# Six projections of a decoder block as seven half-matrix products each, with the weight sums shared by GpSimd and VectorE

## The chip, the core and the metric

The kernel runs on one core of a Trainium2 chip. The metric is the device time of one execution in microseconds (us), as the median of several runs. The engines are TensorE (PE, its weight loads PEld), VectorE (DVE), ScalarE (ACT), GpSimd (POOL) and SyncE (SP), which here only issues DMAs. Each engine works through its own list of instructions in order; semaphores tie the lists together.

## The reference: what is computed

One decoder block for 256 tokens of width 1024, all in float32:

```python
h = rms_norm(x, g_mix)
(qa, ka, va, za, beta, a, qd, kd, vd, gate_a, gate_b) = split(h @ w_in)
oa = gated_delta_rule(l2(silu(conv(qa))), l2(silu(conv(ka))), silu(conv(va)), beta, a)
oa = rms_norm(oa, g_delta_out) * silu(za)
od = rms_norm(diff_attention(norm(qd), norm(kd), vd, lam, rel_bias), g_subln) * (1 - lam_init)
x  = x + (sigmoid(gate_a + b0) * oa + sigmoid(gate_b + b1) * od) @ w_o
x  = x + moe(rms_norm(x, g_ffn))      # top 4 of 32 experts, 1024 -> 2048 -> 1024
```

The change is in the projections qd, kd, vd (attention), za (Z), gate_a and gate_b. Each is h (256 x 1024) times a 1024 x 1024 part of w_in.

## The kernel before, in words

The program has a **front** (all up to the router) and an **expert stage** (32 experts, two per turn of a loop).

Front, first part: 24 *tiles* (L1420) compute q, k and v of the delta rule, transposed, 128 channels at a time; VectorE does the convolution of each tile (L980, L982, L990). Between the last tiles stand the four `kq` steps (L1479 on TensorE; mask products L1067 and L1069 on VectorE).

Front, second part: 48 *half items* `pj` (L1430). Two of them make one quarter result: 128 tokens x 512 columns, eight chunks of 128 channels accumulated in one PSUM bank. A half item is four float32 matmuls, which the profile shows as eight records. They are TensorE's filling: the table `after`, filled by `put(i, ...)`, says which step of the other work each engine does behind item i. The steps that the prediction speaks of:

- `sb`: inversion of 64 triangular 32 x 32 blocks on VectorE, 31 steps of two instructions (L1084, L1085) in eight pieces behind items 3 to 10. At its end (semaphore `s_tc`) SP stores the blocks to DRAM (L496) and loads them back turned (L502, eight DMAs). The first matmuls of the delta rule that use them are `n2` (L1395), behind item 11.
- `nq`, `nk`: the norms of qd and kd on VectorE: a sum over 64 columns (L1115, L1121), a reciprocal, a root on ScalarE, and four small steps (`roots`). `ktd` turns kd on TensorE (L1528); it needs `nk`.
- `y1`, `y2`, `y3`, `yt`, `s1`, `ks`, `o0`, `qs`, `o1`: the delta rule, TensorE L1395, taken by VectorE or ScalarE.
- per attention head h: `a1` (logits; row maximum on VectorE L1182 to L1187, exp on ScalarE L828), `aw` (weights, VectorE L1192 to L1200), `a2` (turn them on TensorE, L1548), `a3` (times the values).
- `odn`, `oan`: norms and gains of both outputs on VectorE; `mt`: turning of the mix; then the four products with w_o (L1574).

SP's queue loads w_in in pieces of 2 MB into ring slots 8, 9 and 6 in turn. As slots of the front die it loads the experts' weights, in slabs of 2 MB: slabs 0 to 4 in the front, 5 to 10 around the product with w_o. From slab 11 on a slab waits until the experts have used the slot (L425). GpSimd has little to do in the front: constants, bias terms, four squares (L643), two squares (L647), and the gain on oa (L652).

Of the kernel before, what the change touches and what calls it, by code (L numbers as in the profile page):

```python
# [11 lines left out]
ALU = mybir.AluOpType  # L12
# [3 lines left out]
P = 128  # L16
# [20 lines left out]
def block_kernel(nc, x, g_mix, w_in, b_gate, conv_w, a_log, dt_bias, g_delta_out, q_norm, k_norm,  # L37
# [17 lines left out]
    NPIECE = 2 * len(GROUPS)  # L55
# [53 lines left out]
    put(9, ("qt", 0))  # L109
    put(10, ("qt", 1), ("nq",))  # L110
# [44 lines left out]
    ROOTS = ["x", "k", "qd", "kd", "oa", "od", "r0", "r1"]  # L155

    ctx = ExitStack()
    with ctx:
# [71 lines left out]
        junk = ring[:, 7, 2 * D:3 * D]  # L230
# [5 lines left out]
        xT = ring[:, 2, 2 * D:].rearrange("p (c t) -> p c t", c=KC)  # L236
        rr_rows = ring[:, 1, 0:T]
# [78 lines left out]
        s_ss, s_tr, s_xT, s_hT = sem("row_squares"), sem("transposes_done"), sem("scaled_xT_blocks_ready"), sem("hT_halves_ready")  # L316
# [4 lines left out]
        s_pj, s_pjf = sem("projections_done"), sem("projections_taken")  # L321
        s_conv, s_sig, s_silu = sem("conv_done"), sem("conv_tanh_done"), sem("silu_done")
# [20 lines left out]
        s_gbl = sem("gate_bias_loaded")  # L343
        s_gs, s_gm, s_gd = sem("gate_tanh_done"), sem("gate_product_done"), sem("gain_product_done")
# [44 lines left out]
        def _(sp):  # L389
# [1414 lines left out]
```

## Time and profile before

| | |
|---|---|
| median of 3 runs | 1275.73 us (1274.88 to 1276.53) |
| span of the profiled execution | 1273.7 us, so 2.0 us below the median |
| TensorE busy | 1229.8 us (97%), granted clock 0.999 of full speed |
| VectorE busy | 373.2 us (29%) |
| ScalarE busy | 284.8 us (22%) |
| GpSimd busy | 45.9 us (4%) |
| DMA | 451.94 MB |
| chain that ended last | TensorE 66%, DMA 19%, VectorE 5%, ScalarE 3% |

The profile is of one execution. Its page gives the busy times, the span in 40 slices, the chain of work that ended last, and the costliest groups of instructions. The whole-span shares mix two stages with different limits, so each stage has to be read by itself. A busy TensorE is not a TensorE at its peak; that a busy share of 97% leaves no idle time says nothing on what each instruction is for.

### The profile page before, as it was taken

The page shows a single profiled execution, that of the slowest core. Times are in us where ns is not written, and L with a number is a line of the kernel's source. Part 1 is how long each engine was busy: PE and PEld are TensorE (multiplying, and loading weights), DVE is VectorE, ACT ScalarE, POOL GpSimd, SP SyncE. Part 2 cuts the span into 40 slices and gives each one's busy share as a digit, 9 for nine tenths or more (in the row PEclk, how much of TensorE's full clock was granted, in tenths as well). Part 3 has the DMA queues.
Part 4 walks back from the last instruction along what each step waited for, and adds up shares of the span by engine and source line. Part 5 has one row for each costly group of instructions (what it writes and reads, how often), then busy time and mean ns, then how long its engine had stood idle before and what let it go on. Part 6 is the DMA issues. An engine that isn't in the chain of part 4 may idle for free.

```text
span 1273.7 us, 14917 instructions
## 1 busy us (share of the span) xinstructions
PE 1229.8 (97%) x5590; PEld 539.1 (42%) x5590; DVE 373.2 (29%) x1063; ACT 284.8 (22%) x573; POOL 45.9 (4%) x100
## 2 busy tenths in 40 slices
PE   9999999999999999999999999999998989999997
PEld 7777466644443333333333333333333333333332
DVE  5766825666231211111221111221111112211111
ACT  3331212352222121121121112121121211121121
POOL 4400000101000000000000000000000000000000
PEclk9999999999999999999999999999999999999999
DMA  7653431567779999999999999999999999999997
GB/s 255 181 164 129 147 134 67 181 248 264 274 284 417 425 429 429 429 428 430 429 428 427 429 428 428 428 429 429 429 428 428 428 428 429 429 429 429 428 427 314
DMA packets 60764, 451.94 MB, mean 355 GB/s; under 512 B 10600, under 2 KB 13800, under 8 KB 36032
## 3 DMA queue, kind: packets, MB, share of 16 engines
q1 hardware_dynamic: 59176, 447.44, 85.2%
q0 software_dynamic: 1120, 3.56, 1.0%
q10 hardware_dynamic: 440, 0.58, 0.1%
q8 instruction: 16, 0.26, 0.1%
q14 instruction: 12, 0.10, 0.0%
HBM read 449.21 MB, written 1.97 MB: 354 GB/s over the span
## 4 chain that ended last, share of the span: by engine, by line
PE 66%; DMA 19%; DVE 5%; ACT 3%; issue 1%; SPq 1%; DVEq 0%; ACTq 0%
PE pb L1719 20%; DMA space<-in_w_up_dram 19%; PE pb L1766 14%; PE pb L1430 11%; PE pb L1660 4%; PE pb L1420 3%; PE pb L1647 3%; PE pb L1574 2%; PE pb L1395 2%; PE pb L1654 1%; PE pb L1679 1%; DVE buf_a L1334 1%; DVE buf_a L1331 1%; DVE buf_a L1328 1%; ACT buf_a L898 1%
## 5 line engine op out<-in xcount | busy, mean ns | idle before, releaser
L1719 PE MATMUL pb<-space,buf_a 128*64 128x512 f32 x2048 | 460.4, 595 | 15.5 <-DMA space<-in_w_up_dram 15.4
L1719 PEld LDWEIGHTS pb<-space,buf_a 128*64 128x64 f32 x2048 | 146.1, 137 | 284.8 <-issue 257.3
L1766 PE MATMUL pb<-space 128*64 128x512 f32 x1024 | 227.1, 595 | 7.3 <-ACT space L905 7.3
L1328 DVE TENSOR_SCALAR buf_a<-pb 128x256 f32<-128x256 f32 x64 | 27.0, 421 | 686.7 <-PE pb L1719 686.7
L1430 PE MATMUL pb<-space 128*128 128x512 f32 x384 | 171.4, 594 | 0.0
L1766 PEld LDWEIGHTS pb<-space 128*64 128x64 f32 x1024 | 70.7, 137 | 140.9 <-issue 125.3
L1430 PEld LDWEIGHTS pb<-space 128*128 128x128 f32 x384 | 70.3, 190 | 76.1 <-issue 75.1
L881 ACT ACT_TABLE_LOAD x32 | 41.1, 1283 | 222.5 <-PE pb L1647 222.5
L1420 PE MATMUL pb<-space 128*128 128x256 f32 x384 | 88.6, 384 | 0.9 <-ACT space L734 0.5
L1420 PEld LDWEIGHTS pb<-space 128*128 128x128 f32 x384 | 71.3, 190 | 13.1 <-issue 2.4
L898 ACT ACTIVATE buf_a<-buf_a 128x256 f32<-128x256 f32 x64 | 26.7, 417 | 216.7 <-DVE buf_a L1328 216.7
L1660 PE MATMUL pb<-space 64*128 64x512 f32 x264 | 65.6, 615 | 0.8 <-ACT space L907 0.8
L907 ACT COPY space<-pb 128x512 f32<-128x512 f32 x32 | 18.7, 585 | 209.8 <-PE pb L1766 209.8
L1647 PE MATMUL pb<-xt,plan 128*64 128x512 f32 x248 | 58.7, 592 | 0.0
L898 ACT ACT_TABLE_LOAD x32 | 41.1, 1283 | 0.6
L905 ACT COPY space<-pb 128x256 f32<-128x256 f32 x64 | 24.4, 382 | 70.1 <-PE pb L1679 70.1
L982 DVE SCALAR_TENSOR_TENSOR space<-space 128x255 f32<-128x255 f32 (+2 forms) x72 | 36.3, 504 | 2.6
L1647 PEld LDWEIGHTS pb<-xt,plan 128*64 128x64 f32 x248 | 18.9, 137 | 34.3 <-issue 34.3
L1660 PEld LDWEIGHTS pb<-space 64*128 64x128 f32 x264 | 22.8, 186 | 23.1 <-issue 23.1
L1395 PEld LDWEIGHTS pb<-space 128*128 128x128 f32 x240 | 29.0, 192 | 6.2 <-issue 6.2
L1331 DVE TENSOR_TENSOR buf_a<-buf_a 128x256 f32<-128x256 f32 x64 | 27.2, 425 | 9.7 <-ACT buf_a L898 6.7
L1334 DVE SCALAR_TENSOR_TENSOR buf_a<-buf_a 128x256 f32<-128x256 f32 x64 | 27.3, 426 | 7.9
(299 smaller groups left out, 807.3 us busy)
## 6 DMA issues: line engine op xcount, KB each, us to landing
space<-in_w_up_dram SPq DMA_DIRECT2D x127, 2048.0 KB, 25.7
space<-in_w_down_dram SPq DMA_DIRECT2D x61, 2048.0 KB, 24.2
space<-in_w_in_dram SPq DMA_DIRECT2D x17, 2048.0 KB, 8.0
space<-in_w_o_dram SPq DMA_DIRECT2D x2, 2048.0 KB, 11.9
space<-in_w_down_dram SPq DMA_DIRECT2D x4, 1024.0 KB, 27.3
space<-in_w_down_dram SPq DMA_DIRECT2D x4, 512.0 KB, 16.0
space<-in_w_up_dram SPq DMA_DIRECT2D x2, 1024.0 KB, 41.1
xt<-in_x_dram SPq DMA_DIRECT2D x2, 512.0 KB, 5.3
```

Of the source, the lines that this page charges most:

```text
L881: sc.copy(xgt, pb[:, 3, :]).then_inc(s_xgt, 1)
L898: sc.activation(sgm[:, 256 * n_:256 * n_ + 256], glu[:, 256 * n_:256 * n_ + 256], ACT.Sigmoid, scale=ALPHA).then_inc(s_sgm, 1)
L1328: v.tensor_scalar(glu[:, cols], pairs[:, :, 0], LIMIT, None, ALU.min).then_inc(s_glu, 1)
L1331: v.tensor_tensor(sgm[:, cols], sgm[:, cols], glu[:, cols], ALU.mult).then_inc(s_mdve, 1)
L1334: v.scalar_tensor_tensor(out=act[:, cols], in0=lin[:, cols], scalar=1.0, in1=sgm[:, cols], op0=ALU.add, op1=ALU.mult).then_inc(s_actv, 1)
L1395: ins = mm(psA[:, h], lhs(h), rhs(h), start=True, stop=True)
L1420: ins = mm(pb[:, t % 2, 0:T], w[:, c, (t % 4) * P:(t % 4) * P + P], rows[:, c, :], start=(c == 0), stop=(c == KC - 1))
L1430: ins = mm(pb[:, q % 2, :], hT[:, c, b * P:(b + 1) * P], piece_at(n)[:, c, :], start=(c == 0), stop=(c == KC - 1))
L1647: ins = mm(pb[64 * n_:64 * n_ + 64, 3, :], sel[:, b, :], xt[:, b, 512 * n_:512 * n_ + 512], start=(b == 0), stop=(b == NB - 1), skip_group ...
L1660: return mm(pb[:, 4 + 2 * b + n_, :], GT[rows, b * P:(b + 1) * P], ys[rows, :], start=False, stop=True, skip_group_check=True)
L1719: ins = mm(up_out(hf, n_), xg[:, c, :], up_columns(line, hf, n_), start=False, stop=(c == KC - 1), skip_group_check=True)
L1766: ins = mm(pb[64 * hf:64 * hf + 64, 2, :], actT[:, c // 4 * 2 + c % 2, hf_in, :], slot(m)[:, at_:at_ + 512], start=(c == 0), stop=(c == KC ...
```

## The change

Each of the six groups is now computed with seven products instead of eight. h is cut into four quarters A11, A12, A21, A22 (128 tokens x 512 channels), the weights into B11, B12, B21, B22 (512 x 512). The products, one *unit* of four matmuls each, in this order: P1 = A11 B11, P5 = SA1 T1, P2 = A12 B21, P6 = SA2 (T1 + B22), P3 = SA4 B22, P7 = SA3 (B12 + B22), P4 = A22 (B21 + T1 + B22), with T1 = B11 + B12 (the two sums are written over B11 and B21). P6 accumulates onto P1 in bank 0, and P3 and P7 onto P5 in bank 7, so a few additions and subtractions give the four quarter results. SA1 to SA4 are sums of quarters of h, made once.

What that brings with it: per group four sums of 128 x 2048 elements, two on GpSimd (`sum_1`, `sum_3`) and two on VectorE (`sum_2`, `sum_4`); four copies out of PSUM on ScalarE and four additions of 128 x 512 on VectorE (`group_result`); gate biases on GpSimd. Squares move from GpSimd to ScalarE, `odn` is split in two. SA1 to SA4 lie in the place of x, so x is loaded a second time (1 MB) for the residual. The loads of w_in become quarters of 1 MB. The table of steps is rewritten for 42 units in place of 48 half items: `nq`, `ktd`, the heads and `mt` stand earlier, `n2` behind 11 as before.

The diff, cut to its core:

```diff
-    put(9, ("qt", 0))
-    put(10, ("qt", 1), ("nq",))
+    put(8, ("qt", 0))
+    put(9, ("qt", 1), ("nq",))
     put(11, ("n2", 0))
     put(12, ("n2", 1))
     put(13, ("y1", 0))
     put(14, ("y2", 0))
-    put(15, ("y3", 0))
-    put(16, ("yt", 0), ("nk",))
-    put(17, ("s1",))
-    put(18, ("ks",), ("ktd", 0))
-    put(19, ("y1", 1), ("ktd", 1))
+    put(15, ("y3", 0), ("nk",))
+    put(16, ("yt", 0), ("ktd", 0))
+    put(17, ("s1",), ("ktd", 1))
+    put(18, ("ks",))
+    put(19, ("y1", 1))
...
-        put(20 + 2 * h, ("a1", h))
-        put(22 + 2 * h, ("aw", h))
+        put(18 + 2 * h, ("a1", h))
+        put(20 + 2 * h, ("aw", h))
...
+            for b in range(NB):
+                sp.dma_start(xt[:, b, :], x[0, b * P:(b + 1) * P, :]).then_inc(s_x[b], 16)
...
+            link(pool.tensor_tensor(SA1, A21, A22, ALU.subtract))
+            link(pool.tensor_tensor(SA2, SA1, A11, ALU.subtract))
+            pool.tensor_tensor(SA3, A11, A21, ALU.subtract).then_inc(s_hT, 1)
+            pool.tensor_tensor(SA4, A12, SA2, ALU.add).then_inc(s_hT, 1)
...
+            def sum_1(g):
...
+                pool.tensor_tensor(quarter(g, "T1"), quarter(g, "B11"), quarter(g, "B12"), ALU.add).then_inc(s_tadd, 1)
+
+            def sum_3(g):
...
+                pool.tensor_tensor(quarter(g, "B12"), quarter(g, "B12"), quarter(g, "B22"), ALU.add).then_inc(s_tadd, 1)
...
+            def sum_2(g):
+
+                dve.wait_ge(s_pj, unit(g, "P1"))
+                dve.wait_ge(s_tadd, 4 * g + 2)
+                v.tensor_tensor(quarter(g, "B11"), quarter(g, "T1"), quarter(g, "B22"), ALU.add).then_inc(s_tadd, 1)
+
+            def sum_4(g):
+
+                dve.wait_ge(s_q("B21"), loaded(g, "B21"))
+                dve.wait_ge(s_pj, unit(g, "P2"))
+                dve.wait_ge(s_tadd, 4 * g + 3)
+                v.tensor_tensor(quarter(g, "B21"), quarter(g, "B21"), quarter(g, "B11"), ALU.add).then_inc(s_tadd, 1)
...
+                if k == 0:
+                    dve.wait_ge(s_pj, unit(g, "P2"))
+                    dve.wait_ge(s_pjf, copied(g, 1))
+                    ins = v.tensor_tensor(dst, pb[:, 1, :], dst, ALU.add)
+                elif k == 1:
+                    dve.wait_ge(s_pj, unit(g, "P3"))
+                    dve.wait_ge(s_pjf, copied(g, 3))
+                    ins = v.tensor_tensor(dst, pb[:, 7, :], dst, ALU.subtract)
+                elif k == 2:
+                    dve.wait_ge(s_pjf, copied(g, 4))
+                    ins = v.tensor_tensor(dst, dst, group_out(g, 3), ALU.subtract)
+                else:
+                    dve.wait_ge(s_pj, unit(g, "P4"))
+                    dve.wait_ge(s_cf, 4 * g + 3)
+                    ins = v.tensor_tensor(dst, pb[:, 1, :], dst, ALU.add)
...
-                elif it[0] == "pj":
+                elif it[0] == "u":
+                    g, name = it[1], UNITS[it[2]]
+                    rows, q, bank = FACTORS[name]
...
+                    for c in range(4):
+                        ins = mm(pb[:, bank, :], rows[:, c, :], cols[:, c, :], start=(opens and c == 0), stop=(c == 3), skip_group_check=True)
+                    ins.then_inc(s_pj, 1)
```

How the lists of instructions change at the places that matter. First VectorE at the end of the inversion, before (L1084 and L1085 are the inversion, the rest is `nq`):

```order
L1084 TENSOR_TENSOR space<-space 64x87 [waits inverse_blocks_started,m_blocks_loaded,dve_chain]
L1085 TENSOR_TENSOR space<-space 64x3x29 [waits dve_chain]
L1084 TENSOR_TENSOR space<-space 64x60 [waits dve_chain]
L1085 TENSOR_TENSOR space<-space 64x2x30 [waits dve_chain]
L1084 TENSOR_TENSOR space<-space 64x31 [waits dve_chain]
L1085 TENSOR_TENSOR space<-space 64x31 [waits dve_chain]
L1115 TENSOR_REDUCE sm<-space 128x32 [waits qd_kd_squared]
L1117 TENSOR_SCALAR sm<-sm 128x32 [waits qd_kd_reduced]
L927 RECIPROCAL sm<-sm 128x32 [waits dve_chain]
L929 TENSOR_TENSOR sm<-sm 128x32 [waits inverse_root_ready]
```

The same place now. L1296 and L1297 are the inversion, L1327 to L1107 are `nq`:

```order
L1297 TENSOR_TENSOR space<-space 64x4x28 [waits dve_chain]
L1327 TENSOR_REDUCE sm<-space 128x32 [waits qd_kd_squared,dve_chain]
L1329 TENSOR_SCALAR sm<-sm 128x32 [waits qd_kd_reduced]
L1102 RECIPROCAL sm<-sm 128x32 [waits dve_chain]
L1104 TENSOR_TENSOR sm<-sm 128x32 [waits inverse_root_ready]
L1105 TENSOR_TENSOR sm<-sm 128x32 [waits dve_chain]
L1106 TENSOR_SCALAR sm<-sm 128x32 [waits dve_chain]
L1107 TENSOR_TENSOR sm<-sm 128x32 [waits dve_chain]
L1296 TENSOR_TENSOR space<-space 64x87 [waits inverse_blocks_started,m_blocks_loaded,dve_chain]
L1297 TENSOR_TENSOR space<-space 64x3x29 [waits dve_chain]
L1296 TENSOR_TENSOR space<-space 64x60 [waits dve_chain]
L1297 TENSOR_TENSOR space<-space 64x2x30 [waits dve_chain]
```

`nq` moved ahead of the last piece of the inversion. A little earlier in VectorE's list, where nothing but the inversion stood before, a weight sum (L1181) and a group result (L1204) of kd now stand between two of its pieces:

```order
L1297 TENSOR_TENSOR space<-space 64x9x23 [waits dve_chain]
L1296 TENSOR_TENSOR space<-space 64x192 [waits dve_chain]
L1297 TENSOR_TENSOR space<-space 64x8x24 [waits dve_chain]
L1181 TENSOR_TENSOR space<-space 128x2048 [waits projections_done,quarter_sums_ready,w_loaded_2,dve_chain]
L1204 TENSOR_TENSOR space<-pb,space 128x512 [waits projections_taken,projections_done]
L1296 TENSOR_TENSOR space<-space 64x175 [waits inverse_blocks_started,m_blocks_loaded]
L1297 TENSOR_TENSOR space<-space 64x7x25 [waits dve_chain]
```

In the same way `sum_2` of kd and three results of qd stand between earlier pieces; `sum_2`, `sum_4` and the first result of qd stand ahead of the inversion.

GpSimd around the same time, before (L635 clears diagonal blocks after the store of the matrix; L643 are squares of kd):

```order
L629 MEMSET space 64x1024
L630 MEMSET space 64x32 [waits pool_chain]
L635 MEMSET space 32x8x32 [waits m_stored,inverse_blocks_started]
L635 MEMSET space 32x8x32 x7
L643 TENSOR_TENSOR space<-space 128x512 [waits projections_taken,qd_kd_reduced,m_diagonal_cleared]
```

The same place now (L760 is `sum_1`, L766 is `sum_3`; groups qd, kd, vd):

```order
L746 MEMSET space 64x1024
L747 MEMSET space 64x32 [waits pool_chain]
L760 TENSOR_TENSOR space<-space 128x2048 [waits w_loaded_0,w_loaded_1,inverse_blocks_started]
L766 TENSOR_TENSOR space<-space 128x2048 [waits quarter_sums_ready,w_loaded_3]
L782 MEMSET space 32x8x32 [waits m_stored,quarter_sums_ready]
L782 MEMSET space 32x8x32 x7
L760 TENSOR_TENSOR space<-space 128x2048 [waits projections_done,w_loaded_0,quarter_sums_ready,w_loaded_1,m_diagonal_cleared]
L766 TENSOR_TENSOR space<-space 128x2048 [waits quarter_sums_ready,w_loaded_3]
L760 TENSOR_TENSOR space<-space 128x2048 [waits projections_done,quarter_sums_ready,w_loaded_0,w_loaded_1]
```

Two large sums of qd now come before the clearing of the blocks, and two of kd behind it, both in the time of the tiles and of the inversion.

## Rows read from the trace of the kernel before

**Rows 1.** Windows: PE, PEld, DVE, ACT, POOL busy (x), clock, DMA share, GB/s.

```profile
372.00:920.00 548.00, 536.34 (x2522) 190.42 (x2520) 99.79 (x304) 109.86 (x180) 0.00 (x0) 1.00 1.00 425
920.00:1263.00 343.00, 320.30 (x1482) 114.61 (x1480) 58.19 (x176) 65.42 (x107) 0.00 (x0) 1.00 1.01 427
```

**Rows 2.** Chain that ended last: start us, length us, what.

```profile
113.83 3.43 PE pb L1430 x8
...
330.07 6.87 PE pb L1574 x16
...
371.72 6.87 PE pb L1719 x32
...
921.85 39.52 DMA space<-in_w_up_dram
```

**Rows 3.** Timeline of SP's queue: start us, length us, instructions.

```profile
151.93 0.49 SPq L496 DMA_DIRECT2D t_blocks<-space  x1
154.82 3.78 SPq L502 DMA_DIRECT2D space<-t_blocks  x8
...
352.52 9.91 SPq L425 DMA_DIRECT2D space<-in_w_up_dram  x2
```

**Rows 4.** Groups by shape, POOL and DVE: busy us, mean ns of one, idle before.

```profile
L652 POOL TENSOR_TENSOR space<-space 128x1024 f32<-128x1024 f32 x2 | 4.7, 2344 | 41.4 <-ACT buf_a L839 41.4
L647 POOL TENSOR_TENSOR space<-space 128x1024 f32<-128x1024 f32 x2 | 3.8, 1893 | 59.3 <-ACT space L712 47.9 <-DVE space L1112 11.4
...
L1115 DVE TENSOR_REDUCE sm<-space 128x32 f32<-128x2048 f32 x1 | 2.3, 2271 | 0.0
L1169 DVE TENSOR_TENSOR space<-pb,space 128x512 f32<-128x512 f32 x8 | 5.5, 692 | 22.6 <-PE pb L1430 22.5
L1146 DVE SCALAR_TENSOR_TENSOR buf_a<-buf_a,sm,space 128x128 f32<-128x128 f32 x16 | 4.3, 347 | 0.0
```

**Rows 5.** Timeline of POOL, two places: start us, length us.

```profile
243.22 1.89 POOL L647 TENSOR_TENSOR space<-space 128x1024 f32<-128x1024 f32 x1 [11.44 <-DVE space L1112]
...
299.30 4.66 POOL L652 TENSOR_TENSOR space<-space 128x1024 f32<-128x1024 f32 x2 [41.41 <-ACT buf_a L839]
```

**Rows 6.** Timeline of DVE at the same places.

```profile
243.26 1.87 DVE L1195 TENSOR_SCALAR sm<-sm 128x2 f32<-128x2 f32 x1
...
301.76 0.69 DVE L1169 TENSOR_TENSOR space<-pb,space 128x512 f32<-128x512 f32 x1 [6.58 <-PE pb L1430]
302.37 2.14 DVE L1002 SCALAR_TENSOR_TENSOR space<-space 128x512 f32<-128x512 f32 x1
```

**Rows 7.** Issues by line, from the page: KB each, median us to landing.

```profile
space<-in_w_in_dram SPq DMA_DIRECT2D x17, 2048.0 KB, 8.0
```

**Rows 8.** Timelines of DVE and PE in the last tiles.

```profile
98.32 0.35 DVE L980 TENSOR_SCALAR space<-space 128x256 f32<-128x256 f32 x1 [1.57 <-ACT space L734]
...
101.76 0.69 DVE L1069 TENSOR_TENSOR space<-space,pb 128x512 f32<-128x512 f32 x1
...
103.21 1.99 PE L1479 MATMUL pb<-space 128*128 128x256 f32 x8
```

**Rows 9.** Timeline of DVE, start and end of the inversion, and `nq`.

```profile
129.07 0.18 DVE L1084 TENSOR_TENSOR space<-space 64x31 f32<-64x31 f32 x1
...
151.82 2.27 DVE L1115 TENSOR_REDUCE sm<-space 128x32 f32<-128x2048 f32 x1
...
158.60 0.19 DVE L929 TENSOR_TENSOR sm<-sm 128x32 f32<-128x32 f32 x1 [3.90 <-ACT sm L686]
```

**Rows 10.** Timeline of PE: the first `n2`.

```profile
159.25 1.95 PE L1395 MATMUL pb<-space 128*128 128x128 f32 x16
```

**Rows 11.** Chain that ended last, one attention head.

```profile
247.63 0.39 DVE space L1182
...
254.05 0.18 DVE sm L1192
...
255.85 1.13 DVE sm L1134
```

More of the change, by code:

```diff
@@ L59, in w_place, with quarter_place @@
         return (8, 9, 6)[n % 3]
+    UNITS = ("P1", "P5", "P2", "P6", "P3", "P7", "P4")
+    U = {name: j for j, name in enumerate(UNITS)}
+    NU = len(UNITS)
+    NG = 6
+    TURN = ((9, 1), (8, 0), (6, 0))
+    def quarter_place(g, q):
+        if q == "B11":
+            return 9, 0
+        if q == "B22":
+            return 8, 1
+        if q == "T1":
+            return (2, 1) if g == 0 else (6, 1)
+        return TURN[(g + (q == "B12")) % 3]
+    OUTS = ((0, 0), (0, 1), (1, 1), (1, 0))
     NSLOT = 11
@@ L147, in block_kernel @@
         sched += extra.get(t, [])
-    for i in range(48):
-        sched.append(("pj", i // 2, i % 2))
+    for i in range(NU * NG):
+        sched.append(("u", i // NU, i % NU))
         sched += after.get(i, [])
@@ new lines, in _ @@
+            sp.wait_ge(s_mst, 16 * 8)
+            sp.wait_ge(s_bup, 1)
+            sp.dma_start(ring[0:64, 0, 0:D], m_dram.ap()).then_inc(s_m32, 16)
+            for q in ("B12", "B11", "B22", "B21"):
+                load_quarter(KD, q)
+            load_quarter(VD, "B12")
+            sp.wait_ge(s_tc, 1)
+            sp.dma_start(t_dram.ap(), Tc_f).then_inc(s_tst, 16)
+            sp.wait_ge(s_tst, 16)
+            sp.wait_ge(s_t0z, 1)
+            for b in range(NB):
+                for d in range(4):
+                    q = 32 * b + 8 * d
+                    sp.dma_start(T0[32 * d:32 * d + 32, b, :, 32 * d:32 * d + 32], bass.AP(t_dram, q * 1024, [[32, 32], [1024, 8], [1, 32]])).then_inc(s_t0[b], 16)
@@ new lines, in _ @@
+            for g in (VD, Z):
+                for q in ("B11", "B22", "B21"):
+                    load_quarter(g, q)
+                load_quarter(g + 1, "B12")
+            load_quarter(GA, "B11")
+            front_dead(0)
+            load(0)
+            load_quarter(GA, "B22")
+            load_quarter(GA, "B21")
+            for i in (1, 2):
+                front_dead(i)
+                load(i)
+            for q in ("B12", "B11", "B22", "B21"):
+                load_quarter(GB, q)
+            sp.wait_ge(s_pj, unit(GA, "P4"))
@@ L504, in _ @@
+            sp.wait_ge(s_tadd, 4 * GB + 1)
+            load_w_o(0, 0)
+            for i in (3, 4):
+                front_dead(i)
+                load(i)
+            sp.wait_ge(s_tadd, 4 * NG)
+            sp.wait_ge(s_pj, unit(GB, "P3"))
+            load_w_o(0, 1)
+            load_w_o(1, 0)
+            sp.wait_ge(s_pj, unit(GB, "P7"))
+            load_w_o(1, 1)
+            for b in range(NB):
+                sp.dma_start(xt[:, b, :], x[0, b * P:(b + 1) * P, :]).then_inc(s_x[b], 16)
             ahead = PERIOD - 1
```

444 lines of the change are left out of this document (274 added, 170 removed).

## The prediction

> **What bounds the kernel now.** I read the windows first, since the shares of the whole span mix two stages. From 372 to 920 us VectorE, ScalarE and GpSimd are mostly idle, TensorE is busy for 536 of 548 us, and the DMA share is already 1.00 at 425 GB/s; from 920 on the DMA share stays at 1.01 and TensorE has idle time [rows 1]. So the transfers are saturated from the start of the expert stage to its end. The chain of waits says the same: from 921.85 us on its long pieces are waits for w_up, the first of 39.5 us [rows 2]. Then the end of the program is the moment at which the saturated stream starts, plus a fixed number of bytes. SP issues slabs 8 and 9 at 352.5 us [rows 3], when products with w_o are done; all later slabs wait for TensorE. A front that ends d us earlier or later moves the whole rest by d. This is the exchange rate I use: one to one. The 1 MB for x costs 1.05 MB / 425 GB/s = 2.5 us of transfer, but it goes out before slab 5, with the DMA engines not yet saturated, and is cost at nothing; without that cover it is 2.5 us.
>
> In the front the chain is nearly all TensorE, from the first projection at 113.83 us to the product with w_o at 330.07 [rows 2]. A half item takes 3.43 us there. So the question is whether the 42 units can run as densely as the 48 half items, with more work on VectorE and GpSimd.
>
> **Removed.** Six units: 6 x 3.43 = 20.6 us off TensorE.
>
> **What one sum costs, and whom it stops.** On VectorE 2048 elements cost 2.27 us (L1115) [rows 4]; no row has two SBUF inputs at this size, so the bounds are 1.5 and 3.0 us, and I take 2.3. An addition of 128x512 with one input in PSUM is 0.69 us. On GpSimd 1024 elements cost 1.89 us for a square of one tile and 2.34 us for two different operands [rows 4]. Doubled, 3.8 to 4.7 us; I take 4.5, since the sums have two different operands. The Trainium skill (GPSIMD Engine Reference, section 3.1) gives 4497 ns for a float32 tensor_tensor of N=2048; no row here has that size.
>
> More matters what stands beside them. While GpSimd ran a square from 243.22 to 245.11 [rows 5], VectorE's L1195, on two elements per partition, took 1.87 us and ended with it [rows 6]. While GpSimd ran L652 from 299.30 to 303.96, L1002 (two SBUF inputs, 128x512) took 2.14 us and ended at 304.51; L1169, with one input in PSUM, took its usual 0.69 us at 301.76, in the midst of the same GpSimd work. So here a VectorE instruction of this kind waits until GpSimd's instruction is over. The Trainium skill (GPSIMD Engine Reference, section 8, Key points) names the same two classes, a 2-port mode or two SBUF inputs; by that rule a GpSimd sum isn't free cover but takes up to its own length from VectorE, and the trace agrees. The inversion (L1084, L1085), the convolution (L980 to L990) and `aw` are of that kind. Bounds of what one GpSimd sum costs VectorE: 0 (VectorE idle or reading PSUM) and 4.7 us.
>
> **Last tiles: +7.4.** B11 of qd is asked for when tile 19 is done, about 92.4 us. A piece of 2 MB lands in 8.0 us [rows 7]; for 1 MB I estimate 5. So `sum_1` runs from 97.6 to 102.1 and `sum_3` behind it to about 106.7. Before, VectorE began a convolution at 98.32 and finished the mask products of the second `kq` at 101.76 + 0.69 = 102.45, in time for TensorE's third `kq` at 103.21 [rows 8]. Now L980 waits for 102.1 and runs its 0.35 us, and the next step waits for 106.95; of the 4.13 us from 98.32 to 102.45 then 3.8 remain: 110.8. TensorE waits 110.8 - 103.2 = 7.6 us, of which 0.2 come back. Bounds 0 (other arrival) and 9.
>
> **The inversion: +23.8.** Count from the first projection (113.83 before). Before, the inversion began at 15.3 (129.07), ran with no gap and ended at 38.0 (151.82) [rows 9]: 22.7 us. Store and reload took until 158.5 at the earliest (the first four of eight loads are out by 156.7 [rows 3], and land some 1.8 us later, an estimate): 6.7 us behind its end. TensorE began `n2` at 159.25, that is 45.5, with about 1 us to spare [rows 10].
> Now: `sum_2`, `sum_4` and one result of qd stand ahead, partly in idle time: start at 18.1. Then 22.7 of inversion; two sums of kd, 4.6; four results, 2.8; GpSimd's two sums of kd, which run in the midst of it once B11 of kd has landed, 9.0; and `nq` ahead of the last piece. `nq` took 151.82 to 159.5 before, with 3.90 us of waiting for ScalarE [rows 9]; with a shorter wait I count 5.3. Sum: 18.1 + 22.7 + 4.6 + 2.8 + 9.0 + 5.3 = 62.5, and 6.8 for the round trip: `n2` at 69.3 instead of 45.5. It is behind item 11 in both lists, so fewer products don't help here: 23.8 us lost. Behind `n2` everything on TensorE is queued, and SP has only the T0 loads in hand, so the weights of vd come later too, but still ahead of TensorE. Bounds: 14 (GpSimd costs nothing) and 27.
>
> **kd norm: +4.6.** `nk` now begins behind `y3` of unit 15 and `ktd` follows one unit and one matmul step later. `nk` takes the 5.3 us of `nq` and 1.2 for the first half of its product (128x1024, half of the 2.3): 6.5 us, and a `y3` step of 1.2 us of the same size stands ahead of it; TensorE has 3.4 for the unit and 1.8 for the matmul step [rows 10]: 2.5 us of wait. Then `sum_4`, a result and `yt` stand behind it on VectorE, and `s1` waits 2.1 us. Bounds 1 and 7.
>
> **Heads: +6.4.** A head takes VectorE and ScalarE 254.05 - 247.63 = 6.4 us from its logits to `aw`, and `aw` 1.8 us [rows 11]. Between the end of a unit and the turning of the weights TensorE has one unit and the next head's logits, 3.4 + some 0.9 = 4.3 us. Where a sum, a result or a gate product (2.3 + 0.7 + 0.7) stand ahead of `aw`, VectorE needs 5.5: 1.2 us of wait, twice, and 1.0 for a logit behind them: 3.4. GpSimd's sums add 3.0 where they hit `aw` or gate products of the last two heads. Bounds 1 and 20 (below, rival 3).
>
> **Tail: +3.4.** Behind the last unit of gate a VectorE has 3.3 us for results and `aw`, 2.8 for the root (`nq` without its long sum, on fewer elements), 12 x 0.347 = 4.2 for `odn` [rows 4], and 3.0 for a gate product and `sum_2`: 13.3, where TensorE has 3 x 3.43 + 1.0 = 11.3 to P6 of gate b, some of it made good: 1.3. The first mix is ready 2.1 us late. Before, the turns stood one whole item ahead of w_o. Bounds 0 and 7.
>
> **Sum.** -20.6 + 7.4 + 23.8 + 4.6 + 6.4 + 3.4 = +25.0 us. Against the profiled span of 1273.7 that is 1298.7; the median lies 2.0 us above that span, so 1300.7. I forecast 1301 us. Idle spells of this length don't occur in the front before, where the granted clock is at its full level, so no row prices a clock that falls from 2.4 to 1.2 GHz in them; I count nothing and keep up to 4 us in the range. The Trainium skill (TensorE: Matmul & The Clock Gate, section on why this matters for your kernels) says that TensorE drops back to half rate when it idles between bursts; by it the sum would be a few us higher.
>
> **Rivals.**
> 1. *GpSimd and VectorE don't hinder each other.* Then the tile term is 0, the inversion 14.7 (TensorE still waits for `nq` and for the interleaved sums), the heads 3.4: -20.6 + 14.7 + 4.6 + 3.4 + 3.4 = +5.5 with overlaps of 1 to 2 us: about 1280. Against it: rows 5 and 6. Chance 0.14.
> 2. *Faster: TensorE stays the bound.* The price is the 20.6 us, less what is left of the inversion. It decides at the time the inverse is stored: if that is under 39 us behind the first projection, `n2` doesn't wait. For it: some waits of mine may overlap, and VectorE waited for TensorE before the inversion. If half of the terms vanish: 1264 to 1272. Against it: the inversion had no gap, and `nq` moved ahead of its end. 1268, chance 0.12.
> 3. *VectorE becomes the bound in the heads too.* Each of the eight GpSimd sums of vd to gate b takes its whole 4.5 us from VectorE, 36 us where I count 3; with VectorE half idle, some 18 stay: 1316. For it: results and gate products are of the kind that waits. Against it: most of `a1` reads PSUM. Chance 0.14.
> 4. *The waits are there but shorter,* since one hides the next: half of 25 us: 1288. It is within the likeliest case's own range, 1286 to 1309.
>
> The likeliest has 0.56; between it and the cases of gain lie 0.04 for no change. A difference under 0.2% (2.6 us) can't be told from none. Faster: 0.13, all of rival 2 and a little of 1; same 0.07, where 1 and 2 meet; slower 0.80. The range leaves out the better half of rival 2 and the end of rival 3: 1271 to 1314.
>
> **What would show it.** In the profile after: on TensorE an idle time of over 10 us before the first `n2`, released by the loads of T0 (the step of 23.8; under 5 us it is wrong); the inversion stretched to over 40 us, with L1296 or L1297 rows of 4 us beside L760 and L766 on GpSimd; about 7 us of wait before the third `kq`; a wait of TensorE for VectorE at the first `ktd`; GpSimd sums of 4 to 4.7 us; and the first expert about 25 us later than 371.7 [rows 2], with the expert stage's windows unchanged. An expert stage of another length would break the one-to-one rate.

## The result: 1328.7 us, 4.2% slower than before, and the profile after

The changed kernel takes 1328.74 us (median of 4 runs, 1327.94 to 1330.56) where the kernel before took 1275.72. The ratio is 1.0416, 95% interval 1.0401 to 1.0431. The sign was right. The forecast of 1301 and its range up to 1314 were too low: +25 us forecast, +53 measured.

The page of the kernel after, busy time of the engines and the line of the granted clock (40 slices of the span, tenths of full speed):

```profile
PE 1225.8 (92%) x5542; PEld 538.9 (41%) x5542; DVE 450.3 (34%) x1083; ACT 300.2 (23%) x606; POOL 110.0 (8%) x119
...
PEclk9998979998899999999999999999999999999999
```

GpSimd has 8% of the span and yet, as the runs below show, costs more than any other part of the change. Before, every digit of the clock was 9.

The two stages that answer to [rows 1], 53.1 us later (columns as there):

```profile
425.10:973.10 548.00, 536.39 (x2522) 190.48 (x2520) 99.71 (x304) 109.87 (x180) 0.00 (x0) 1.00 1.00 425
973.10:1316.10 343.00, 320.19 (x1480) 114.99 (x1476) 58.15 (x176) 65.44 (x107) 0.00 (x0) 1.00 1.01 427
```

The expert stage is the same in every column: all of the loss arises before it and moves it whole. The chain that ended last, to be read against [rows 2]:

```profile
104.33 3.73 DVE space L1155
...
178.89 16.61 issue
...
334.85 6.96 DVE space L1416 x2
...
974.92 39.76 DMA space<-in_w_up_dram
```

Before, the front of this chain was nearly all PE. Now VectorE instructions stand in it for many times their usual length, and 16.61 us in which TensorE waits ahead of `n2`. For these the profile names no releaser ("issue"); that they end with the store and reload of the inverse is shown by e4 below, where the store goes out 4.7 us earlier and `n2` follows.

TensorE's own timeline shows where (the bracket is the idle time before the row):

```profile
68.72 5.41 PE L1638 MATMUL pb<-space 128*128 128x256 f32 x16 [3.88 <-ACT space L910]
...
116.12 3.78 PE L1723 MATMUL pb<-space 128*128 128x256 f32 x8 [6.84 <-DVE space L1281]
...
195.50 3.50 PE L1613 MATMUL pb<-space 128*128 128x128 f32 x16 [16.61 <-issue]
...
252.61 3.28 PE L1613 MATMUL pb<-space 128*128 128x128 f32 x16 [2.36 <-DVE space L1309]
...
312.98 0.88 PE L1792 MATMUL pb<-ident,space 128*128 128x128 f32 x3 [6.72 <-ACT buf_a L1014]
313.65 5.79 PE L1675 MATMUL pb<-space 128*128 128x512 f32 x8
...
341.87 0.90 PE L1792 MATMUL pb<-ident,space 128*128 128x128 f32 x3 [6.45 <-DVE space L1416]
342.56 4.99 PE L1675 MATMUL pb<-space 128*128 128x512 f32 x8
...
355.72 0.90 PE L1792 MATMUL pb<-ident,space 128*128 128x128 f32 x3 [3.67 <-DVE space L1416]
356.41 4.90 PE L1675 MATMUL pb<-space,xt 128*128 128x512 f32 x8
```

`n2` (the row at 195.50) started at 159.25 before [rows 10].

The timeline of GpSimd after:

```profile
60.61 1.44 POOL L735 TENSOR_TENSOR xt<-space,xt 128x512 f32<-128x512 f32 x1
...
103.38 4.51 POOL L760 TENSOR_TENSOR space<-space 128x2048 f32<-128x2048 f32 x1 [35.61 <-DMA space<-in_w_in_dram]
...
151.02 4.54 POOL L760 TENSOR_TENSOR space<-space 128x2048 f32<-128x2048 f32 x1 [15.14 <-DMA space<-in_w_in_dram]
...
332.38 4.65 POOL L800 TENSOR_TENSOR space<-space 128x1024 f32<-128x1024 f32 x2 [1.98 <-ACT space L960]
336.99 4.67 POOL L760 TENSOR_TENSOR space<-space 128x2048 f32<-128x2048 f32 x1
```

The timeline of VectorE in the same kernel:

```profile
58.09 4.25 DVE L1157 SCALAR_TENSOR_TENSOR space<-space 128x255 f32<-128x255 f32 x3
...
104.33 3.72 DVE L1155 TENSOR_SCALAR space<-space 128x256 f32<-128x256 f32 x1 [1.58 <-ACT space L910]
108.08 5.77 DVE L1157 SCALAR_TENSOR_TENSOR space<-space 128x255 f32<-128x255 f32 x3
...
151.23 4.53 DVE L1296 TENSOR_TENSOR space<-space 64x175 f32<-64x175 f32 x1
155.79 4.61 DVE L1297 TENSOR_TENSOR space<-space 64x175 f32<-64x175 f32 x1
...
183.83 2.29 DVE L1327 TENSOR_REDUCE sm<-space 128x32 f32<-128x2048 f32 x1
...
189.18 0.18 DVE L1297 TENSOR_TENSOR space<-space 64x31 f32<-64x31 f32 x1
...
334.85 6.96 DVE L1416 SCALAR_TENSOR_TENSOR space<-space,sm 128x256 f32<-128x256 f32 x2
```

`sum_3` (L766, 4.5 us) follows `sum_1` (L760) at 108.04 and 155.71. Each GpSimd instruction has a VectorE row of about its own length beside it. L1155 takes 0.35 us alone [rows 8] and 3.72 here; two L1416 take 0.75 us together alone and 6.96 here, across the gain product (L800) and the first sum of gate b (L760). The inversion's last step is at 189.18, behind `nq` (from 183.83); the store, the reload (issued at 192.30) and so `n2` follow.

For all comparisons I cut the front at four moments of TensorE: the first `kq`, the first projection P1, `n2`, and the first product with w_o (92.43, 113.67, 159.25 and 329.90 us before). The table says by how much each stage is longer than before, in us, from the profiled execution of each kernel. Two kernels with the same work ahead of the first `kq` differ there by up to 1.6 us, so that column is no finer than this.

| kernel | to kq | kq to P1 | P1 to n2 | n2 to w_o | all |
|---|---|---|---|---|---|
| after | +6.0 | +8.9 | +21.4 | +16.8 | +53.1 |
| e1 GpSimd sums narrow | +5.6 | 0.0 | +13.6 | +2.5 | +21.6 |
| e7 all sums narrow | +6.6 | 0.0 | +8.9 | -7.2 | +8.4 |
| e2 sums by VectorE | +6.0 | 0.0 | +22.2 | +7.8 | +36.0 |
| e3 x sums by VectorE | +0.2 | +9.2 | +21.5 | +17.0 | +47.9 |
| e4 nq behind | +5.6 | +8.6 | +17.4 | +17.2 | +48.8 |
| e6 slab 0 behind | +5.1 | +8.8 | +21.6 | +14.4 | +49.9 |
| e9 sums in four | +5.4 | +4.7 | +20.8 | +9.5 | +40.3 |
| e5 before, four sums | +1.4 | 0.0 | +9.0 | +2.4 | +12.8 |

### The profile page after: what moved, and what is told of

Read it like the earlier page. It is cut to its first block, busy times and chain, and to the rows that moved or that the text cites. A ratio compares the mean times of both kernels' runs of the same rounds, so it can differ in the third digit from the quotient of the medians.

```text
span 1327.0 us, 14985 instructions
## 1 busy us (share of the span) xinstructions
PE 1225.8 (92%) x5542; PEld 538.9 (41%) x5542; DVE 450.3 (34%) x1083; ACT 300.2 (23%) x606; POOL 110.0 (8%) x119
## 4 chain that ended last, share of the span: by engine, by line
PE 57%; DMA 19%; DVE 11%; issue 4%; ACT 3%; SPq 1%; POOL 0%; DVEq 0%; ACTq 0%; POOLq 0%
PE pb L1960 20%; DMA space<-in_w_up_dram 19%; PE pb L2007 14%; PE pb L1675 5%; PE pb L1901 4%; PE pb L1638 3%; PE pb L1888 3%; PE pb L1815 2%; PE pb L1613 2%; PE pb L1895 1%; PE pb L1920 1%; DVE buf_a L1549 1%; DVE buf_a L1552 1%; DVE buf_a L1546 1%; ACT buf_a L1073 1%
## 5 line engine op out<-in xcount | busy, mean ns | idle before, releaser
L1675 PE MATMUL pb<-space,xt 128*128 128x512 f32 x192 | 87.4, 603 | 0.5 <-DVE space L1174 0.5
L1638 PEld LDWEIGHTS pb<-space 128*128 128x128 f32 x384 | 72.8, 194 | 17.2 <-ACT space L910 4.2
L1675 PE MATMUL pb<-space 128*128 128x512 f32 x144 | 68.5, 622 | 0.0
L1675 PEld LDWEIGHTS pb<-space,xt 128*128 128x128 f32 x192 | 35.7, 193 | 39.9 <-issue 39.3
L1613 PE MATMUL pb<-space 128*128 128x128 f32 x240 | 32.2, 292 | 20.4 <-issue 16.6
L1157 DVE SCALAR_TENSOR_TENSOR space<-space 128x255 f32<-128x255 f32 (+2 forms) x72 | 43.4, 603 | 2.6
L1613 PEld LDWEIGHTS pb<-space 128*128 128x128 f32 x240 | 31.3, 207 | 27.1 <-issue 21.7
L1675 PEld LDWEIGHTS pb<-space 128*128 128x128 f32 x144 | 27.8, 202 | 29.4 <-issue 29.0
L760 POOL TENSOR_TENSOR space<-space 128x2048 f32<-128x2048 f32 x6 | 27.3, 4557 | 137.8 <-DMA space<-in_w_in_dram 137.8
```

The lines of the kernel that those rows point to most:

```text
L760: pool.tensor_tensor(quarter(g, "T1"), quarter(g, "B11"), quarter(g, "B12"), ALU.add).then_inc(s_tadd, 1)
L1157: ins = v.scalar_tensor_tensor(out=a[:, d:], in0=src[:, 0:T - d], scalar=conv_c[:, 3 - d, tap:tap + 1], in1=a[:, d:], op0=ALU.mult, op1=AL ...
L1613: ins = mm(psA[:, h], lhs(h), rhs(h), start=True, stop=True)
L1638: ins = mm(pb[:, t % 2, 0:T], w[:, c, (t % 4) * P:(t % 4) * P + P], rows[:, c, :], start=(c == 0), stop=(c == KC - 1))
L1675: ins = mm(pb[:, bank, :], rows[:, c, :], cols[:, c, :], start=(opens and c == 0), stop=(c == 3), skip_group_check=True)
```

## The experiments

Theory A: a VectorE instruction that works from SBUF to SBUF stands still until the running GpSimd instruction is over, and TensorE waits behind VectorE. Rival B: VectorE's own added work. Rival C: late weight loads through SP's order.

**e5: the kernel before, with four idle sums on GpSimd.** The hindrance by itself, without any part of the change.

```
 pool.wait_ge(s_off, 1)
+pool.wait_ge(s_t5, 16 * (P // COPIES))
+for i in range(4):
+    pool.tensor_tensor(ring[:, 2, 2 * D:], ring[:, 3, 2 * D:], ring[:, 1, 2 * D:], ALU.add).then_inc(s_dum, 1)
+    pool.wait_ge(s_dum, i + 1)
...
 elif it == ("n2", 0):
+    dve.wait_ge(s_dum, 4)
```

VectorE's added wait stands in its step of `n2`, long after the four sums are over (at 141.43), so it holds nothing up.

> The kernel before, with four additions of 128x2048 added to GpSimd (two different operands, result used by nobody and overwritten), started behind its memset at about 121.7 us; they run to about 140, so 10.7 us of them lie beside the inversion. The computation stays. Theory A (a VectorE instruction with two SBUF inputs waits for the whole GpSimd instruction): the inversion gets stretched by about 10 us, with single rows L1084 or L1085 (now some lines later) of up to 4.5 us instead of 0.2 to 0.3, the inverse is stored that much later, n2 loses 9 us and some 1.6 to the clock: 1286 us. Rival B (they don't hinder each other): 1276 us, the inversion stays 22.7 us long.

Measured 1288.1 us, ratio 1.0094 (1.0078 to 1.0111). GpSimd's timeline of this run:

```profile
123.08 18.35 POOL L641 TENSOR_TENSOR space<-space 128x2048 f32<-128x2048 f32 x4
```

VectorE's timeline in the same run:

```profile
123.84 2.16 DVE L1015 TENSOR_SCALAR space<-pb,sm 128x128 f32<-128x128 f32 x8 [2.15 <-PE pb L1497]
...
130.42 1.82 DVE L1089 TENSOR_TENSOR space<-space 64x31 f32<-64x31 f32 x1
132.28 0.20 DVE L1090 TENSOR_TENSOR space<-space 64x31 f32<-64x31 f32 x1
132.52 4.39 DVE L1089 TENSOR_TENSOR space<-space 64x60 f32<-64x60 f32 x1
136.95 4.56 DVE L1090 TENSOR_TENSOR space<-space 64x60 f32<-64x60 f32 x1
```

From 130.42 on, 11.0 us of GpSimd's sums are left, and three rows grow by 10.2 us together; the inversion takes 33.0 us (130.42 to 163.41) for 22.7 [rows 9]. The row that reads PSUM (pb) keeps its 2.16 us in the midst of it. That is theory A, and rival B's time of 1276 is refuted. Between two of these GpSimd instructions one or two VectorE instructions get through. The Trainium skill (SBUF — State Buffer, section "SBUF: two separate sides") calls the port pair of the two engines an exclusive lock, held for the whole instruction; by that rule this trace agrees, with 4.56 us for an instruction of 0.2.

**e1: GpSimd's sums narrow.** `sum_1` and `sum_3`:

```
-pool.tensor_tensor(quarter(g, "T1"), quarter(g, "B11"), quarter(g, "B12"), ALU.add)
+pool.tensor_tensor(quarter(g, "T1")[:, 0:64], quarter(g, "B11")[:, 0:64], quarter(g, "B12")[:, 0:64], ALU.add)
```

> Leaves out most of GpSimd's sums of weight quarters (64 of 2048 columns are added, so the factors of P5, P6, P7 and P4 are wrong). Theory A (GpSimd's sums hold VectorE, and TensorE waits behind it): the last tiles give back about 8.9 us, the inversion 9.0, the heads and the tail some 12: 1299 us; no row of VectorE on two SBUF inputs stretches to 4.5 us beside GpSimd any more, except beside the four additions of x sums and the bias additions. Rival B (VectorE's own added work decides, not the hindrance): the inversion stays at +21 us, 1324 or more. Rival C (late weight loads decide in the heads): last tiles and inversion give back 18, but the waits of 6.7 and 6.5 us in the heads stay: 1311.

Measured 1296.7 us, ratio 1.0153 (1.0136 to 1.0170). Theory A's 1299 holds, to 2.3 us; B (1324) and C (1311) don't. 54 us of GpSimd work (twelve sums, about 4.5 each), on an engine that is idle most of the time, cost 32 us. VectorE at the place of 104.33 and 108.08 above:

```profile
103.88 0.35 DVE L1155 TENSOR_SCALAR space<-space 128x256 f32<-128x256 f32 x1 [1.57 <-ACT space L910]
104.27 1.52 DVE L1157 SCALAR_TENSOR_TENSOR space<-space 128x255 f32<-128x255 f32 x3
```

**e7: VectorE's sums narrow as well** (`sum_2` and `sum_4` cut to `[:, 0:64]` in the same way).

> All 24 sums of weight quarters cut to 64 of 2048 columns, on GpSimd and on VectorE (the factors of P5, P6, P7 and P4 are wrong). Against the run with only GpSimd's sums narrow (1296.7): the four VectorE sums of qd and kd that stand ahead of or in the inversion go, 4 x 2.2 us: 1288 us; the heads give 1 or 2 more: 1286. The rest above before is then nq ahead of the inversion's end, the nine results, the x sums and the slow clock, against the six products saved. If VectorE's sums were covered by waiting: 1296.

Measured 1282.9 us, ratio 1.0051 (1.0034 to 1.0067). Against e1 the inversion's stage gains 4.6 us, where I expected 8.8, and the stage behind it 9.7, where I expected 1 or 2: VectorE's sums are not covered in the heads. Even with all weight sums nearly free the kernel is slower than before. It still has the four sums of x on GpSimd (5.8 us, e3) and `nq` ahead of the end of the inversion (4.0 us, e4); without these two it would be about level with before, an estimate from these figures that no run tests.

**e2: the twelve sums of GpSimd done by VectorE.**

```
-pool.tensor_tensor(quarter(g, "T1"), quarter(g, "B11"), quarter(g, "B12"), ALU.add)
+v.tensor_tensor(quarter(g, "T1"), quarter(g, "B11"), quarter(g, "B12"), ALU.add)
...
+if g < GB and name == "P7":
+    sum_1(g + 1)
+elif g < GB and name == "P4":
+    sum_3(g + 1)
```

> The whole computation stays; the twelve sums of weight quarters that GpSimd did (4.5 us each) are done by VectorE (2.3 us each). Theory A: in the last tiles nothing is left of the wait before the third kq (-8.9 us), the inversion is 4.4 us shorter (2 x 2.3 for 2 x 4.5), the heads gain some 8: about 1307 us. Rival B: VectorE has 27.6 us more to do, and it decides: 1329 to 1345.

Measured 1311.4 us, ratio 1.0268 (1.0251 to 1.0285). VectorE gets 27 us more to do and the program is 17 us shorter, so rival B falls. The last tiles and the heads gain as expected, the inversion nothing: it now starts 22.3 us behind P1 (141.97 against 119.70) for 18.1, since the two sums of qd stand ahead of it, and this takes back what its two undisturbed sums give.

**e9: the same sums as four instructions each.**

```
-pool.tensor_tensor(quarter(g, "T1"), quarter(g, "B11"), quarter(g, "B12"), ALU.add)
+for i in range(4):
+    c = slice(512 * i, 512 * i + 512)
+    pool.tensor_tensor(quarter(g, "T1")[:, c], quarter(g, "B11")[:, c], quarter(g, "B12")[:, c], ALU.add)
```

> The whole computation; each of GpSimd's twelve sums of 128x2048 is issued as four of 128x512 in a row. Theory A, in its finer form from e5 (at the end of each GpSimd instruction exactly one waiting VectorE instruction gets through): VectorE gets four instructions through per sum instead of one, so the inversion gains 2 x 3 x 0.35 = 2 us, the last tiles about as much, the heads 2 to 3: 1321 to 1323 us; the stretched rows are about 1.2 us instead of 4.5. Rival (the hindrance is shared bandwidth, in proportion to the bytes): no change, 1328 to 1330, since the bytes are the same.

Measured 1316.1 us, ratio 1.0310 (1.0294 to 1.0326): 12 to 13 us for an edit that leaves the work as it is, twice what I expected. GpSimd's timeline in the inversion:

```profile
146.11 5.37 POOL L761 TENSOR_TENSOR space<-space 128x512 f32<-128x512 f32 x4 [15.05 <-DMA space<-in_w_in_dram]
```

VectorE's timeline in the same run:

```profile
146.40 1.28 DVE L1300 TENSOR_TENSOR space<-space 64x175 f32<-64x175 f32 x1
147.72 1.29 DVE L1301 TENSOR_TENSOR space<-space 64x175 f32<-64x175 f32 x1
```

One VectorE instruction per GpSimd instruction, whatever its size. The sum takes 5.4 us for 4.5, but the unit of waiting falls from 4.5 to 1.3. Bytes are the same and the time is not, so the rival, a hindrance in proportion to the bytes, is refuted. The gain lies in the last tiles (4.2) and behind `n2` (7.4), where VectorE has a few instructions to finish for TensorE; in the long row of the inversion it is 0.6, less than the 2 expected.

**e3: the sums of x by VectorE**, one behind each of tiles 13 to 16.

```
-link(pool.tensor_tensor(SA1, A21, A22, ALU.subtract))
...
+if it[1] == 13:
+    link(v.tensor_tensor(SA1, A21, A22, ALU.subtract))
```

> The four additions that make the left factors from x go from GpSimd, where they run beside the tiles at 56 to 62 us, to VectorE, one behind each of tiles 13 to 16. Theory A: the 3.9 us of idle TensorE before the tile at 68.7 us and its slow clock go, and the first kq comes 6 us earlier: 1323 us. Rival: that delay comes from other work there (ScalarE's copies): 1329.

Measured 1325.4 us, ratio 1.0381 (1.0364 to 1.0398). The medians are 3.3 us apart, and the interval ends just below that of after (1.0398 against 1.0401). The stage tells more: the first `kq` is back at 92.63, and the tile that began at 68.72 after 3.88 us of idle time now reads:

```profile
64.60 3.72 PE L1641 MATMUL pb<-space 128*128 128x256 f32 x16 [0.47 <-ACT space L904]
```

So four additions of 1.3 us on GpSimd cost 5.8 us in this stage, give or take the 1.6 by which it varies. They stood in no term of my sum.

**e4: nq one unit later,** behind the last piece of the inversion.

```
-    put(9, ("qt", 1), ("nq",))
+    put(9, ("qt", 1))
+    put(10, ("nq",))
```

> nq goes one unit later, behind the last piece of the inversion. Theory A: the inverse is stored 4.5 to 5.3 us earlier, and everything behind n2 comes that much earlier: 1324 us. Rival: the wait moves elsewhere (ScalarE's squares of kd wait for nq, and the copies of the results behind them), so that TensorE or nk is late again: 1328 to 1331.

Measured 1324.9 us, ratio 1.0374 (1.0356 to 1.0391). Its stage gives back 4.0 us, TensorE's wait before `n2` falls from 16.61 to 12.63, and nothing of it returns in the stage behind.

**e6: slab 0 behind gate a's quarters.**

```
 load_quarter(GA, "B11")
-front_dead(0)
-load(0)
 load_quarter(GA, "B22")
 load_quarter(GA, "B21")
-for i in (1, 2):
+for i in (0, 1, 2):
```

> SP issues the quarters B22 and B21 of gate a ahead of slab 0, which waits for the end of the state's last product. Theory C (the 6.7 us wait of TensorE at 313 us stems from that order: GpSimd waits for B22 and starts its sum on top of the gate products): the wait shrinks to under 2 us and the program by 4 to 6: 1323 to 1325 us. Rival (VectorE is simply late with the work in front of it): 1328, the wait stays or turns up one head later.

Measured 1326.1 us, ratio 1.0397 (1.0380 to 1.0415): not told apart from after. TensorE where the 6.72 us stood:

```profile
296.81 0.55 PE L1790 MATMUL pb<-ident,space 128*128 128x128 f32 x3 [1.20 <-DVE space L1414]
...
303.26 0.80 PE L1800 MATMUL pb<-space 128*128 128x128 f32 x2 [2.47 <-ACT space L876]
...
312.06 0.52 PE L1790 MATMUL pb<-ident,space 128*128 128x128 f32 x3 [1.83 <-ACT buf_a L1012]
...
317.55 0.49 PE L1800 MATMUL pb<-space 128*128 128x128 f32 x2 [1.54 <-ACT space L876]
```

The one wait falls to 1.83 as theory C says, and 5.2 us of smaller ones appear beside it (after, 2.3 stood there: 0.66 and 1.65), so the waits are 7.0 us together for 9.0. The unit behind the one that shrank takes 3.60 us for 5.79. The stage gains 2.4 us, not the 4 to 6 of theory C. The late load placed the wait; 7.0 of the 9.0 us come from the work in front of it.

**e8: five edits at once, the state later.** e2, e3, e4 and e6 together, and the chain from `n2` to `o1` four units later, so that the inverse's store and reload have cover.

```
+    put(14, ("nk",))
+    put(15, ("n2", 0), ("ktd", 0))
+    put(16, ("n2", 1), ("ktd", 1))
+    put(17, ("y1", 0))
...
-            load_quarter(VD, "B12")
+            for q in ("B12", "B11", "B22", "B21"):
+                load_quarter(VD, q)
```

> The whole computation, and five places changed at once: sums by VectorE as in e2 (1311.4 us), x sums by VectorE as in e3 (-3.3), nq one unit later, slab 0 behind gate a's quarters, and the state's chain from n2 to o1 four units later (the loads of vd's quarters ahead of the store of the inverse). Theory A: the 16.7 us of wait before n2 and 1.6 us of slow clock go, another 1.5 from slab 0: 1289 us. Rival: the later chain collides with the heads on VectorE and turns up as waits of a1 and a2: 1295 to 1305.

Measured 1295.2 us, ratio 1.0148 (1.0131 to 1.0165), at the edge of the rival. The wait before `n2` is gone, and 4.50 us (ScalarE's copy, stuck behind `nq`), 3.98 (`nk`) and 8.35 us (the last `aw`) appear.

**e10: VectorE's list rearranged on top of e8.**

```
+        put(NU * g, ("ws", 2, g))
+        put(NU * g + 2, ("ws", 4, g))
...
-        after[i].sort(key=lambda it: {"aw": 0, "a2": 0, "a1": 2}.get(it[0], 1))
+        after[i].sort(key=lambda it: {"aw": 0, "a2": 0, "a1": 2, "gp": 3, "ws": 4}.get(it[0], 1))
```

> The whole computation, as in e8 (1295.2 us), with VectorE's list rearranged: the weight sums and gate products stand behind the weights of a head (aw) in the same unit instead of ahead of them, sum_3 and sum_2 of qd behind the first transposes of v, nq ahead of the last piece of the inversion again, and the transposes of kd one unit later. If all that is left of the loss are waits of TensorE for VectorE's order, the waits of 3.2, 4.5, 4.0 and 8.4 us of e8 and 3 us of slow clock go: 1270 to 1274 us, faster than before (1276). Rival: VectorE is the bound there, and each wait comes back at the next step: 1285 to 1295.

Measured 1287.3 us, ratio 1.0093 (1.0078 to 1.0107): the best full version, and still slower than before. The time is the rival's. Up to `n2` VectorE has hardly any room (busy 61.0 of the 70 us from 115 to 185, as much as TensorE with 60.8), and TensorE waits 2.63 and 3.28 us for `sum_2` of qd and kd. One wait comes from SP's queue:

```profile
173.41 0.75 SPq L591 DMA_DIRECT2D t_blocks<-space  x1
184.44 3.78 SPq L597 DMA_DIRECT2D space<-t_blocks  x8
```

The inverse's store took 11.0 us until the reload could go, for 2.9 both in after (189.39 to 192.30) and before [rows 3]: it went out right behind a quarter of 1 MB.

**e11: e10 with three sums back on GpSimd, in fours, and sum_2 ahead of sum_3.**

```
-    put(NU * g - 1, ("ws", 3, g))
+    put(NU * g + 2, ("ws", 3, g))
...
+                if VD <= g < GB:
+                    sum_1(g + 1)
```

> The whole computation, as in e10 (1287.3 us), with two changes: sum_2 is done ahead of sum_3 and the latter two units later (P6 needs the one, P7 the other), and sum_1 of z, gate a and gate b is done by GpSimd in four pieces. If the waits of TensorE for sum_2 (2.6, 3.3 and 3.5 us in e10) are a matter of order: 9 us less there, of which 6 come back before n2, where VectorE has no idle time: 1281 to 1284 us. If GpSimd's pieces cost VectorE what they take off it: the heads gain nothing. Rival: VectorE is the bound up to n2 and order doesn't help: 1287. Faster than before (1276) in neither case.

Measured 1294.5 us, ratio 1.0132 (1.0114 to 1.0149): slower than e10, a miss. GpSimd's timeline:

```profile
306.55 4.95 POOL L774 TENSOR_TENSOR space<-space 128x512 f32<-128x512 f32 x4 [12.61 <-DMA space<-in_w_in_dram]
311.46 1.26 POOL L765 TENSOR_TENSOR plan<-plan,space 128x512 f32<-128x512 f32 x1
312.68 4.64 POOL L803 TENSOR_TENSOR space<-space 128x1024 f32<-128x1024 f32 x2
```

TensorE's timeline in the same run, a little later:

```profile
318.50 0.90 PE L1813 MATMUL pb<-ident,space 128*128 128x128 f32 x3 [7.57 <-DVE space L1437]
```

VectorE's timeline ahead of it:

```profile
312.76 0.69 DVE L1233 TENSOR_TENSOR plan<-pb,plan 128x512 f32<-128x512 f32 x1 [6.34 <-POOL plan L765]
```

Sum, bias and gain product stand in a row for 10.8 us just where the last `aw` has to get through. Most of this wait is not the hindrance: the bias addition (L765) stands behind the sum in GpSimd's own list, a result on VectorE needs it and idles 6.34 us, and `aw` stands behind that result. Two edits were made at once. Up to `n2` only the order of the sums differs, and this stage is as long as in e10 (74.15 us for 73.99), so the 6 us expected there didn't come; behind `n2` e11 is 7.9 us longer, and how much each edit has of that stays open.

## Why the forecast failed

**Right: the exchange rate, the unit prices and the mechanism.** The first expert moved by 53.1 us and the span by 53.3. A GpSimd sum takes 4.5 us, forecast 4.5; one of VectorE 2.29, forecast 2.3. That VectorE stands still beside GpSimd was read from [rows 5, 6] and is shown by e5.

**Nearly right: last tiles, +7.4, measured +8.9.** The wait is 6.84 us for the 7.6 counted; the half clock behind it, counted as nothing, adds 2.0 (`kq` 3.78 us for 1.99, the next tile 3.81 for 3.62). **The inversion, +23.8, measured +21.4.** It starts 18.1 us behind P1 and takes 42.8, forecast 18.1 and 44.4. GpSimd's sums have 7.8 of the loss (after against e1; forecast 9.0) and `nq` 4.0 (e4; 5.3). VectorE's four have 4.6 (e1 against e7), where the forecast had more: 4.6 for the two inside and most of the 2.8 of the later start.

**The rivals.** Rival 1 (no hindrance) falls with e5, rival 2 (TensorE stays the bound) with the 16.6 us before `n2`, rival 4 (shorter waits) with the total. Rival 2 also had a slip: the five terms of loss add up to 45.6 us, and half of them against the 20.6 saved is +2.2, so 1278, not 1264 to 1272.

**Missing: the sums of x.** The sum has no term for them. I weighed the twelve long sums and passed over four of 1.3 us in the tiles. They cost 5.8 us (e3): the convolution of a tile is four dependent VectorE instructions, each of which met one GpSimd instruction.

**Wrong: the term "Heads: +6.4", and in it the step "GpSimd's sums add 3.0 where they hit `aw` or gate products of the last two heads".** This is the mis-sized term. From `n2` to w_o I forecast +14.4 of waits against -20.6 of removed units; measured is +37.4. TensorE's own waits in this stage are 27.1 us: 2.8 for the norm of kd (forecast 4.6), 21.5 in the heads and the steps of the delta rule between them (6.4) and 2.7 in the tail (3.4). By cause, the 37.4 are 14.3 for GpSimd's sums (after against e1), 9.7 for VectorE's (e1 against e7), and 13.4 of other things. Of these 13.4, e7 still shows 10.2 as seven waits of 0.7 to 2.0 us (before had one, 0.6) and 2.6 as slow clock behind `n2`; which of results, gate products, squares and roots makes each wait wasn't taken apart.

Where GpSimd's sums cost TensorE time, the lag of after behind e1 shows, followed row by row from `n2` on. It shrinks by 1.4 us just behind `n2` and then grows at four places only: by 4.2 at the step of 252.61 (`sum_3` of z, from 243.80), by 3.9 at the fifth head (312.98, `sum_3` of gate a), and by 3.9 and 3.7 at the last two heads (341.87 and 355.72, the sums of gate b). So the last two heads alone cost 7.6 where I had 3.0, and two places that I had not counted cost 8.1. The sums at 203.57, 208.30, 236.26 and 283.95 cost TensorE nothing. Even a tiny instruction is held. The one below (0.17 us in e1) delays an exp and a copy on ScalarE, and so the step of 252.61:

```profile
245.12 3.22 DVE L1403 TENSOR_SCALAR sm<-sm 128x4 f32<-128x4 f32 x1
```

Rival 3 named this loss and gave 18 us for it; the 14.3 are nearer to its figure than to mine, though half of the eight sums cost nothing. A price near it belonged in the sum.

**Too small: the clock, counted as nothing, with up to 4 kept in the range.** Windows of after, with the granted clock in the third column from the right:

```profile
116.00:120.00 4.00, 3.88 (x9) 3.16 (x10) 2.26 (x7) 0.00 (x0) 0.00 (x0) 0.50 0.00 0
...
313.00:319.00 6.00, 6.00 (x11) 2.94 (x12) 3.17 (x8) 4.43 (x14) 0.89 (x1) 0.58 0.45 167
```

After an idle time of 6.84 us TensorE runs at 1.2 GHz (0.50 of 2.4) for the 4 us of the first window. Against the usual 3.72, 1.99, 1.95, 1.95, 3.60, 3.60 and 3.60 us, the seven long rows behind waits shown above (5.41, 3.78, 3.50, 3.28, 5.79, 4.99, 4.90) are 11.2 us longer. The waits ahead of them were 2.36 to 16.61 us long, and each cost 1.3 to 2.2 us more in this way. Behind a wait of 1.41 us the next row took 2.05 us for 1.95. These 11.2 us lie inside the stages above and below, not beside them.

**The account.** Over the forecast: x sums 6.0, last tiles 1.4, inversion -2.4, `n2` to w_o 23.0; together 28.0, and 25.0 + 28.0 = 53.0. Of the 23.0, 11.3 are GpSimd's sums (14.3 for 3.0).

## What to carry to other kernels

Idle time of GpSimd is no free place for SBUF arithmetic while VectorE has short dependent steps that TensorE waits for: count every such instruction at its full length against VectorE, and then see whether TensorE waits for what stands behind it (here 54 us of such sums cost 32). If it must be there, issue it in small pieces, which gave back 12 us here; whether gaps between the pieces help more wasn't tested. See also what stands behind it in GpSimd's own list (e11). Fewer products on TensorE pay only if the engines that prepare the factors have room: with all weight sums nearly gone, but those of x and the early `nq` left, the same schedule was still 0.5% slower than before, and the best full version, with every sum on VectorE and its list reordered, 0.9%. Add the price of the slow clock to every wait of TensorE as long as those above, and look at what a small transfer on the critical path stands behind (11.0 us for 2.9 in e10); sending it first is untried here.

## What the runs showed of the hardware that I had not expected

- The two engines take turns by instruction: beside back-to-back GpSimd instructions VectorE gets about one through per instruction, of 4.5 us or of 1.3 (e5, e9). That makes splitting worth 12 us here.
- One SBUF input is enough to be held: a TENSOR_SCALAR of 128x256 took 3.72 us for 0.35, and one of four elements per partition 3.22 for 0.17. A TENSOR_REDUCE of 128x1024 from SBUF wasn't (the first row here; GpSimd's L766 ran from 301.38 to 305.90 and held the second):

```profile
301.78 1.22 DVE L1346 TENSOR_REDUCE sm<-space 128x8 f32<-128x1024 f32 x1 [2.57 <-ACT space L954]
302.92 3.54 DVE L1190 SCALAR_TENSOR_TENSOR space<-space 128x512 f32<-128x512 f32 x1
```

- The hindrance works in both directions: in e8 GpSimd's bias addition took 3.42 us at 309.08, beside a sum of 2.29 us on VectorE that began at the same time, for 1.26 alone.
